# One attention-and-gate loop of an encoder kernel: value products of high and low parts side by side, keys of two heads in one product, and the gate's norm spread over three engines

## What is computed

```python
h = rmsnorm(x, norm_mix_g[l])
proj = h @ w_in[l]
h_q, h_kv, k_pe, h_sg = proj[..., :c1], proj[..., c1:c2], proj[..., c2:c3], proj[..., c3:]
o_mla = mla_mixer(h_q, h_kv, k_pe, ...)      # 8 heads, keys 64 + 32 wide, values 64 wide, softmax over 512 keys
o_sg = spatial_gating_mixer(h_sg, ...)       # z = gelu(h_sg); u, v = halves of 512; v = layernorm(v)
                                             # mixed = einsum('hij,bcjhd->bcihd', w_s, v) + b_s; u * mixed
o = concat([rmsnorm(o_mla), rmsnorm(o_sg)])
x = x + o @ w_out[l]
```

## Time and profile before

| | us |
|---|---|
| median of 3 runs | 1498.18 (1496.62 to 1498.19) |
| the profiled execution, device time | 1497.97 |
| its span, first to last instruction | 1496.2 |
| PE busy in the span | 1460.7 (98%) |
| DVE, ACT, POOL busy | 748.4, 692.1, 646.5 |

### The profile page before, as it was taken

How to read it: one execution, slowest core, us unless ns; L and a number is a source line. 1 busy time by engine, 2 the same in 40 slices (tenths; PEclk the granted TensorE clock), 3 DMA queues, 4 the chain that set the end, 5 groups by cost and what they waited for, 6 DMA issues and landing times.

```text
span 1496.2 us, 19445 instructions
## 1 busy us (share of the span) xinstructions
PE 1460.7 (98%) x6876; PEld 1196.7 (80%) x6876; DVE 748.4 (50%) x1154; ACT 692.1 (46%) x1107; POOL 646.5 (43%) x313
## 2 busy tenths in 40 slices
PE   8999999999999999999999999999999999999996
PEld 7776689888888888888878776888888888888884
DVE  7648578343355420445264776781526544024534
ACT  6566746354354421344355775553534444124432
POOL 2433148644343554354445322684343454435350
PEclk9999999999999999999999999999999999999998
DMA  5320225412233333232323102453031332323231
GB/s 204 101 82 15 70 82 158 143 56 71 61 106 101 112 99 99 85 104 80 121 80 98 55 29 71 127 183 99 29 99 57 113 112 81 116 85 100 77 91 57
DMA packets 38888, 138.75 MB, mean 93 GB/s; under 512 B 4448, under 2 KB 4704, under 8 KB 38560
## 3 DMA queue, kind: packets, MB, share of 16 engines
q1 hardware_dynamic: 37872, 134.25, 29.3%
q10 hardware_dynamic: 944, 3.51, 0.7%
HBM read 135.64 MB, written 2.10 MB: 92 GB/s over the span
## 4 chain that ended last, share of the span: by engine, by line
PE 74%; issue 10%; DVE 8%; ACT 4%; POOL 4%; DMA 0%; SPq 0%; POOLq 0%; DVEq 0%; ACTq 0%
PE ps L1387 24%; PE ps L1388 24%; PE ps L1389 24%; POOL w_lo L358 4%; DVE small L1085 1%; ACT work L606 1%; DVE h_lo L1111 1%; DVE arena L1111 1%; DVE work L1170 0%; PE ps L1543 0%; DMA raw<-blocks_d 0%; DVE arena L1067 0%; ACT arena L614 0%; DVE work L1062 0%; DVE work L1097 0%
## 5 line engine op out<-in xcount | busy, mean ns | idle before, releaser
L358 POOL TENSOR_TENSOR w_lo<-raw,w_hi 128x1024 fp32r<-128x1024 f32 x244 | 594.5, 2454 | 704.4 <-ACT w_hi L459 704.4
L1387 PE MATMUL ps<-h_hi,w_hi 128*128 128x512 f32 (+1 forms) x1040 | 406.0, 390 | 3.5 <-DVE w_lo L900 1.7
L459 ACT ACTIVATE w_hi<-raw 128x1024 fp32r<-128x1024 f32 x247 | 255.0, 1054 | 330.8 <-PE ps L1389 327.8
L1389 PE MATMUL ps<-h_hi,w_lo 128*128 128x512 f32 (+1 forms) x1040 | 403.1, 388 | 0.0
L1388 PE MATMUL ps<-h_lo,w_hi 128*128 128x512 f32 (+1 forms) x1040 | 403.1, 388 | 0.0
L1387 PE MATMUL ps<-arena,w_hi 128*128 128x512 f32 (+2 forms) x656 | 244.3, 372 | 4.4 <-DVE work L1062 2.4
L1389 PE MATMUL ps<-arena,w_lo 128*128 128x512 f32 (+2 forms) x656 | 241.9, 369 | 0.0
L1388 PE MATMUL ps<-arena,w_hi 128*128 128x512 f32 (+2 forms) x656 | 241.8, 369 | 0.0
L1387 PEld LDWEIGHTS ps<-h_hi,w_hi 128*128 128x128 f32 x1040 | 195.2, 188 | 47.3 <-issue 3.1
L1388 PEld LDWEIGHTS ps<-h_lo,w_hi 128*128 128x128 f32 x1040 | 195.3, 188 | 40.6 <-issue 1.0
L1389 PEld LDWEIGHTS ps<-h_hi,w_lo 128*128 128x128 f32 x1040 | 195.2, 188 | 40.1
(11 more groups left out here) (185 smaller groups left out, 1780.7 us busy)
## 6 DMA issues: line engine op xcount, KB each, us to landing
raw<-blocks_d SPq DMA_DIRECT2D x247, 512.0 KB, 3.5
work<-memT_d ACTq DMA_DIRECT2D x2, 1024.0 KB, 4.9
outT_d<-work SPq DMA_DIRECT2D x8, 256.0 KB, 2.2
x<-xT_d SPq DMA_DIRECT2D x3, 512.0 KB, 7.5
work<-ln_d ACTq DMA_DIRECT2D x2, 512.0 KB, 3.6
x<-xT_d SPq DMA_DIRECT2D x2, 256.0 KB, 4.5
raw<-blocks_d SPq DMA_DIRECT2D x2, 256.0 KB, 4.9
par<-par_d ACTq DMA_DIRECT2D x2, 113.5 KB, 3.9
```

Of the source, the lines that this page charges most:

```text
L358: gp.tensor_tensor(w_lo[:, b % SPLIT, :], raw[:, b % RAW, :], w_hi[:, b % SPLIT, :].bitcast(F32), ALU.subtract).then_inc(lo_done.sem, 1)
L459: act.activation(w_hi[:, b % SPLIT, :], raw[:, r, :], ACT.Copy).then_inc(hi_done.sem, 1)
L1387: pe.matmul(out, a_hi, b_hi, start=first, stop=False)
L1389: return pe.matmul(out, a_lo, b_hi, start=False, stop=last)
```

## The change

The values' high and low parts are interleaved by head (`v_pair`), so that 128 columns of weights hold both. Per key tile `attend` then issues two products, high-and-low by high (128 columns, both halves of bank 3) and high by low (64 columns). ACT copies the upper half of the bank to `part` (`copy_part`), DVE adds the lower half to it and multiplies by the spread sums. `spread_sums` moves to t = 2.

`k_proj(p)` makes the keys of two heads in one product of 128 columns, in bank 2 instead of 4 (p > 0), at t = 0 of even heads. ACT takes the even head's high part and a plain copy of the odd head's keys (`k_odd`); the odd head's high part is made from that copy by ACT, its low part by POOL (`key_low`).

The layer norm of v: the mean comes from the accumulator of the gelu, the variance from four ACT squares with the mean as bias; DVE does one step per tile (subtract mean, times root), POOL multiplies by the gain and adds the bias (`gate_norm`). The scaling of the gate moves from ACT to DVE, all four tiles at step (6, 3); squares and root of the gate move from head 5 to head 6; the mixes move from heads 3 and 4 to heads 4 and 5, partly into bank 4; the blocks of the last head pair and of w_s change places.

```diff
-B_HEAD = (B_WV + 1, B_V + 4, B_V + 5, B_V + 7)
-B_WS = B_V + 6
+B_HEAD = (B_WV + 1, B_V + 4, B_V + 5, B_V + 6)
+B_WS = B_V + 7
...
-STAT_STEPS = ((0, 1), (0, 2), (0, 3), (1, 0))
-ROOT_STEP = (1, 1)
-NORM_STEPS = ((1, 2), (1, 3), (2, 2), (2, 3))
-SPLIT_STEPS = ((1, 3), (2, 0), (2, 3), (3, 0))
-
-MIX_STEPS = ((3, 2), (3, 3), (4, 2), (4, 3))
-
-GATED_STEPS = ((5, 0), (5, 1), (5, 1), (5, 2))
-GATED_ROOT = (5, 3)
-SCALED_STEPS = {(6, 1): (0, 1), (6, 2): (2, 3)}
+STAT_STEPS = ((0, 1), (0, 2), (0, 2), (0, 3))
+ROOT_STEP = (1, 0)
+NORM_STEPS = ((1, 0), (1, 1), (1, 2), (1, 3))
+SPLIT_STEPS = ((2, 0), (2, 1), (2, 2), (2, 3))
+
+MIX_STEPS = ((4, 1), (5, 0), (5, 1), (5, 3))
+
+GATED_STEPS = ((6, 0), (6, 0), (6, 1), (6, 1))
+GATED_ROOT = (6, 2)
+SCALED_STEPS = {(6, 3): (0, 1, 2, 3)}
...
-        v_hi, v_lo = arena[:, 8:12, :], arena[:, 12:16, :]
+        v_pair = arena[:, 8:16, :].rearrange("p (k a) n -> p k (a n)", k=TT).rearrange("p k (h s d) -> p k h s d", s=2, d=VD)
+        v_hi, v_lo = v_pair[:, :, :, 0, :], v_pair[:, :, :, 1, :]
...
-        rsum = work[0:64, 11, :]
+        part = work[0:64, 11, :]
...
-        def k_bank(h):
-            return (5, 7)[h] if h < 2 else 4
+        def k_bank(p):
+            return 5 if p == 0 else 2
+
+        def mix_bank(n):
+            return 2 if n == 1 else 4
...
+                def key_low(p):
+                    need(kh_done, 2 * p + 2)
+                    gp.tensor_tensor(k_lo[0:64, 1, :], k_odd[:, :], k_hi[0:64, 1, :].bitcast(F32), ALU.subtract)\
+                        .then_inc(kodd_done.sem, 1)
+
+                def gate_norm(t):
+                    need(vs_done, t + 1)
+                    gp.tensor_tensor(vt[:, t, :], vt[:, t, :], ln_gb[:, 0, :], ALU.mult).then_inc(vg_mul.sem, 1)
+                    need(vg_mul, t + 1)
+                    gp.tensor_tensor(vt[:, t, :], vt[:, t, :], ln_gb[:, 1, :], ALU.add).then_inc(vn_done.sem, 1)
+
...
-                for h in range(HEADS):
-                    if h == 3:
-                        gate_low(3)
-                    if h % 2 == 1:
-                        low(B_V + 7 + h // 2)
-                    if h + 2 < HEADS:
-                        query_low(h + 2)
-                    for g in {1: (0,), 2: (1, 2)}.get(h, ()):
-                        gate_low(g)
+                query_low(2)
+                low(B_V + 7)
+                query_low(3)
+                key_low(1)
+                need(ln_in, 16)
+                gate_norm(0)
+                gate_norm(1)
+                query_low(4)
+                gate_norm(2)
+                gate_low(0)
+                gate_norm(3)
+                for t in range(1, TT):
+                    gate_low(t)
+                query_low(5)
+                key_low(2)
+                low(B_V + 8)
+                query_low(6)
+                query_low(7)
+                key_low(3)
...
-                def k_part(h):
-                    if h % 2 == 0:
-                        need(kp_mm, h // 2 + 1)
-                    else:
-                        block_used(B_HEAD[h // 2])
-                    act.activation(k_hi[0:64, h % 2, :], ps[k_bank(h)][0:64, :], ACT.Copy).then_inc(kh_done.sem, 1)
+                def k_even(p):
+                    block_used(B_HEAD[p])
+                    act.activation(k_hi[0:64, 0, :], ps[k_bank(p)][0:64, :], ACT.Copy).then_inc(kh_done.sem, 1)
+                    if p > 0:
+                        need(kodd_done, p)
+                    act.activation(k_odd[:, :], ps[k_bank(p)][64:128, :], ACT.Copy).then_inc(kst_done.sem, 1)
+
+                def k_second(p):
+                    need(kst_done, p + 1)
+                    act.activation(k_hi[0:64, 1, :], k_odd[:, :], ACT.Copy).then_inc(kh_done.sem, 1)
...
-                def copy_sums(h):
-                    need(spread, h + 1)
+                def copy_part(h):
+                    need(pv_mm, h + 1)
                     if h > 0:
                         need(o_done, h)
-                    act.activation(rsum, ps[sum_bank(h)][0:64, :], ACT.Copy).then_inc(rsum_done.sem, 1)
+                    act.activation(part, ps[B_PV][64:128, :], ACT.Copy).then_inc(part_done.sem, 1)
...
+                    if t == 3 and h >= 1:
+                        copy_part(h - 1)
                     turned_hi(i)
...
+                    for c in range(TT):
+                        if (h, t) == STAT_STEPS[c]:
+                            need(vmean, 1)
+                            act.activation(sv_hi[:, c, :], vt[:, c, :], ACT.Square, bias=nmean[:, c:c + 1],
+                                           accum_out=vsq[:, c:c + 1]).then_inc(vsq_done.sem, 1)
...
-                    for c in SCALED_STEPS.get((h, t), ()):
-                        need(gated_root, 1)
-                        act.activation(u[:, c, :], u[:, c, :], ACT.Copy, scale=sm_t[:, c:c + 1])\
-                            .then_inc(sg_normed.sem, 1)
...
-                def k_part(h):
-                    need(kh_done, h + 1)
-                    dve.tensor_tensor(k_lo[0:64, h % 2, :], ps[k_bank(h)][0:64, :], k_hi[0:64, h % 2, :].bitcast(F32),
+                def k_even(p):
+                    need(kh_done, 2 * p + 1)
+                    dve.tensor_tensor(k_lo[0:64, 0, :], ps[k_bank(p)][0:64, :], k_hi[0:64, 0, :].bitcast(F32),
                                       ALU.subtract).then_inc(kl_done.sem, 1)
...
                 def attended(h):
 
-                    need(rsum_done, h + 1)
-                    need(pv_mm, h + 1)
-                    dve.tensor_tensor(o_mla[64 * (h % 2):64 * (h % 2) + 64, h // 2, :], ps[B_PV][0:64, :], rsum, ALU.mult)\
-                        .then_inc(o_done.sem, 1)
+                    need(part_done, h + 1)
+                    dve.tensor_tensor(part, ps[B_PV][0:64, :], part, ALU.add).then_inc(whole_done.sem, 1)
+                    need(whole_done, h + 1)
+                    need(spread, h + 1)
+                    dve.tensor_tensor(o_mla[64 * (h % 2):64 * (h % 2) + 64, h // 2, :], ps[sum_bank(h)][0:64, :], part,
+                                      ALU.mult).then_inc(o_done.sem, 1)
...
-                def statistics(src, t):
-                    link(dve.bn_stats(bn[:, t, :], src[:, t, :]))
-                    dve.sem_inc(dve_passed, 1)
-                    link(dve.bn_aggr(mv[:, t, :], bn[:, t, :]))
...
+                    if t == 1 and h % 2 == 0 and h + 2 < HEADS:
+                        k_even((h + 2) // 2)
...
+                    turned_lo(i)
                     if t == 3 and h >= 1:
                         attended(h - 1)
-                    turned_lo(i)
                     if t == 2:
...
-                    if (h, t) in STAT_STEPS:
-                        c = STAT_STEPS.index((h, t))
-                        need(vg_done, c + 1)
-                        statistics(vt, c)
-                        if c == TT - 1:
-                            dve.tensor_scalar(sm_v, mv[:, :, 1], EPS, None, ALU.add).then_inc(s_v.sem, 1)
-                    if (h, t) == NORM_STEPS[0]:
+                    if i == 0:
+                        need(vg_done, TT)
+                        dve.tensor_scalar(nmean, vsum, -1.0 / SG, None, ALU.mult).then_inc(vmean.sem, 1)
+                    if (h, t) == ROOT_STEP:
+                        need(vsq_done, TT)
+                        dve.tensor_scalar(sm_v, vsq, 1.0 / SG, EPS, ALU.mult, ALU.add).then_inc(s_v.sem, 1)
                         small_root(1)
-                        need(ln_in, 16)
                     if (h, t) in NORM_STEPS:
                         g = NORM_STEPS.index((h, t))
-                        link(dve.scalar_tensor_tensor(out=vt[:, g, :], in0=vt[:, g, :], scalar=mv[:, g, 0:1],
-                                                      in1=ln_gb[:, 0, :], op0=ALU.subtract, op1=ALU.mult))
-                        dve.scalar_tensor_tensor(out=vt[:, g, :], in0=vt[:, g, :], scalar=sm_t[:, g:g + 1],
-                                                 in1=ln_gb[:, 1, :], op0=ALU.mult, op1=ALU.add).then_inc(vn_done.sem, 1)
+                        dve.tensor_scalar(vt[:, g, :], vt[:, g, :], nmean[:, g:g + 1], sm_t[:, g:g + 1], ALU.add, ALU.mult)\
+                            .then_inc(vs_done.sem, 1)
 
...
                         small_root(2)
-                        dve.sem_inc(gated_root.sem, 1)
+                    for c in SCALED_STEPS.get((h, t), ()):
+                        dve.tensor_scalar(u[:, c, :], u[:, c, :], sm_t[:, c:c + 1], None, ALU.mult).then_inc(sg_normed.sem, 1)
...
                     if h >= 2:
-                        need(kl_done, h)
+                        need(qf_done, h)
+                        if h == HEADS - 1:
+                            need(gated, 2)
...
-                def k_proj(h):
-                    b = B_HEAD[h // 2]
+                def k_proj(p):
...
-                    if h >= 2:
-                        need(qf_done, h + 1)
-                    else:
-                        need(vl_done, 2 * h + 2)
```

(50 more changed lines are left out.)

## The result

| | before | after |
|---|---|---|
| median of the runs, us | 1497.4 (1496.26 to 1498.19, 4 runs) | 1510.69 (1510.12 to 1511.36, 4 runs) |
| ratio, 95% interval | | 1.009 (1.0072 to 1.0107) |
| span of the profiled execution, us | 1496.2 | 1508.8 |
| mean granted clock of TensorE | 0.996 | 0.988 |

The account below looks back on a forecast made before the run. The loop was taken as TensorE-bound for six heads, then following ScalarE and VectorE. Per layer -0.7 - 0.7 - 2.6 + 5.3 + 0.5 - 0.9 = +0.9, two layers +1.8: forecast 1500.0 us, own range 1497 to 1503, wider range 1484 to 1506.

Parts of the forecast that it names:

- Head start and work behind the loop: Before and behind the head loop: 3 and 4 fewer TensorE products gain 0.7 and 0.9 us per layer.
- the first and the last term: Products saved before the loop (0.7 us) and behind it (0.9 us), claimed as gained because TensorE streams on both sides.
- Heads 0 to 2: First three heads of the loop: TensorE saves 2.5 us, but head 3 starts only 1.4 earlier, 0.7 from head start: gain 0.7.
- they are level: Heads 0 to 2: ScalarE's busy time becomes 28.2 us and TensorE's 27.5, so the two were called level.
- Heads 3 to 5: Middle heads of the loop: TensorE saves 4.1 us, the stretch takes 30.5 us instead of 33.1: gain 2.6 per layer.
- Heads 6 and 7: Last two heads: the gate's chain sets the time, 22.3 us for 17.0, a loss of 5.3 per layer.
- Both waits for GpSimd: Heads 6 and 7: VectorE's root steps and scalings of the gate wait for GpSimd's block subtractions, 4.3 us per layer together.
- The clock: Inside the loop: a TensorE stand of 6 us can lower its clock; taken as 0.5 us lost per layer.
- rival 3: Clock falls ahead of the gate's transposes and stays down to loop's end: 2 to 4 us per layer, about 1506; chance 0.20.
- Terms of PE: 44 fewer matmuls per layer, 0.23 us apart: 10.1 us per layer, 20.2 in all.
- rival 4: 128-column products or ScalarE's strided value write cost more than their like, saved matmuls worth half: 1510; chance 0.05.
- Rival 2: TensorE-bound throughout: stretches keep their old idle time and all 88 saved matmuls count, 1477.8 us; chance 0.12.

Follow-up runs that it names:

- e13: The norm's redistribution alone on the kernel before, plus 8 value products per head for 12, low part of values left out of the output: 1485.86 us, ratio 0.9923.
- e9: Kernel before with the norm's redistribution and the values' pairing, keys as before, gate's products at heads 4 and 5: 1499.88 us, ratio 1.0017.
- e2: Changed kernel with the keys of heads 4 and 5 made in the queries' bank, so they don't wait for the first head's output: 1512.08 us, ratio 1.0101.
- e17: e11 with VectorE's low part of the even key one step later, at (0,2) and (2,2): 1503.24 us, ratio 1.0040.
- e7: Kernel before with the norm and its statistics redistributed, values and keys as before: 1491.51 us, ratio 0.9953.
- e14: e7 with the keys of two heads made in one product, in the queries' bank, values as before: 1494.39 us, ratio 0.9982.
- e1: Changed kernel with two weight blocks split at other steps, so GpSimd's block subtractions miss the gate's root and scalings: 1505.04 us, ratio 1.0053.
- e3b: Changed kernel with 26 useless products ahead of the gate's first transpose and 8 before the second, filling TensorE's stand: 1507.0 us, ratio 1.0071.
- e11: Changed kernel with the gate's steps earlier, its products all in bank 2, the last keys in bank 4: 1504.39 us, ratio 1.0048.
- e3: Changed kernel with 20 useless products ahead of the gate's first transposes, which left part of TensorE's stand empty: 1510.79 us, ratio 1.0094.

## Why the prediction was wrong

Total: forecast +0.9 per layer, measured +6.3 in the profiled spans (12.6 for two).

- **Head start and work behind the loop** (-0.7, -0.9). Measured -0.6 from the first loop's end to the second's first turn (651.66 for 652.28) and -0.2 behind the second loop; the first layer's first turn came 1.1 us earlier (93.65 for 94.71), but profiled starts vary by 2.5 us. Together -1.0 per layer, 0.6 short. The step "the first and the last term have PE streaming on both sides, so they are gained" fails for the first: from the same product of the second layer (at 779.13 before, 784.59 after) to its first turn it takes 49.07 and 49.05 us, with three products fewer in it. TensorE now waits there for ScalarE's four gelus of the gate (TensorE after and before, ScalarE after, first layer):

```profile
68.36 0.50 PE L1427 MATMUL ps<-w_hi,h_hi 128*128 128x512 f32 x1 [0.75 <-ACT work L621]
69.41 0.50 PE L1387 MATMUL ps<-w_hi,h_hi 128*128 128x512 f32 x1
...
65.88 2.42 ACT L621 ACTIVATE work<-ps,small 128x512 f32<-128x512 f32 x4
```

  The price of a product behind the loop was right (e13: 0.9 us for four). With the output made in two steps 0.3 of it is lost again (e9 against e13), within the 0.5 that the prediction allowed.
- **Heads 0 to 2** (-0.7): measured +2.4. The largest miss, 3.1 per layer. The failing step is "they are level", worked out from busy times summed over three heads and taken as the stretch's length. The sums themselves came out (PE busy 27.66 us and ACT 27.47, for 27.5 and 28.2), but in a stretch of 33.48 us. It also reckoned the key's wait for an output with the last pair only and missed that of heads 4 and 5, 3.26 us; but e2 shows that knowing it would have led to the wrong price too, as its removal gave nothing.
- **Heads 3 to 5** (-2.6): measured -2.0 and -2.3. Right within 0.6. But time moves between these stretches (e2, e17), so heads 0 to 5 are better taken as one: forecast -3.3, measured +0.2. By the runs with parts the norm gives -3.6 there (e7), the keys on top of it +1.5 (e14) and the values on top of it +2.1 (e9), which add up to it within 0.2. So the 29 products of TensorE counted there as a gain of 6.6 us cost 3.8 with the copies and second steps that came with them.
- **Heads 6 and 7** (+5.3, and +0.5 for the clock): measured +6.8 and +7.3, the clock included. Both waits for GpSimd stand where they were put, and the gate's chain is what TensorE waits for; taking both waits away gave 3.2 us, not 4.3, as ScalarE's copy is next. But the rest of the chain was reckoned too short: without the waits the forecast's own sum is 18.0 us, and e1 took 20.9 (its clock, at 0.84 there, has a share in that). The Trainium skill's sentence in "GPSIMD Engine Reference", section Key points, on interfaces shared with VectorE agrees: 2.01 us beside GpSimd, 0.16 without.
- **The clock** (+0.5): 1.4 to 1.7, shown by e3b. Mis-sized by the factor of three; rival 3 named the mechanism at 2 to 4 us and 1506.
- **Terms of PE**: 10.1 us per layer counted. The matmuls start 0.23 us apart as forecast and rival 4 is out, though its 1510 is near the measured time; but a product inside the loop is worth under a quarter of that. Rival 2 (1477.8) fell for this reason.
- **What no step had**: each part by itself. The sum took the three parts as one. By the runs: norm -7.0 us; keys +0.7 alone, +4.3 on the norm; values +9.4 alone, +9.6 on the norm, of which the products are -4.5 and their output +14. The whole change and values with norm differ by 10.9 us: 4.6 of that is left when the gate's products stand as early as the bank allows (e11 against e9), for the keys and for the scalings on VectorE; 6.3 goes with the gate's place (e11 against the changed kernel), the waits for GpSimd there included.

I had rated VectorE's second output step "0.84 + 0.60 for 0.60" and let it vanish in a busy sum (27.6 for 26.3 of 33 us), though VectorE's steps are what TensorE's three largest waits ended with the earlier trace rows. That was in the profile, and it pointed to this.

## What to carry to other kernels

Split a change of several parts and price each alone: here a part worth -7 us was hidden under two that together cost more. In a loop where engines hand tiles to each other every 2.5 us, a wait's length is no price and a product's length isn't either; what the runs point to is how many steps the engines that release TensorE have in each short window, so look at which list is full in windows of a head, not of three. And less work for TensorE can mean a stand that lowers its clock.

## What the hardware showed that I had not expected

Time removed from one head came back in the next almost to the tenth of a us: 1.11 and 1.11 us in e17, 1.09 and 1.11 in the second layer of e3. Useless products made the kernel 2.8 us faster, by the clock alone. And the same kernel can keep or lose the clock in the same place from layer to layer: in head 2 of e3 (14.00 and 12.91 us), which changed nothing at the end of head 3, and in head 3 of e9 (12.59 and 11.24 us), which left 0.9 us at the end of head 5.
